# The first weight panel in two transfers, and the first product ahead of the second half of x

## The reference

```python
h = rmsnorm(x, norm_mix[0])
b_gate, c_gate, u = jnp.split(h @ w_in, 3, axis=-1)    # w_in: 1024 x 3072
v = c_gate * u
conv = causal convolution of v over 3 tokens
x = x + (b_gate * conv) @ w_out
```

## Time and profile before

| what | value |
|---|---|
| median of 3 runs | 1274.33 us (1272.78 to 1274.46) |
| profiled execution, its own time | 1270.87 us |
| its span in the trace | 1269.1 us |
| TensorE busy | 1236.7 us, 97% of the span |
| VectorE, ScalarE busy | 1001.9 us, 844.2 us |
| bytes moved | 325.22 MB, mean 256 GB/s |

### The profile page before, as it was taken

One profiled execution on the slowest core, in us unless ns is written; L12 is line 12 of the kernel. 1 busy time (PEld: TensorE's weight loads), 2 busy tenths in 40 slices (PEclk: granted clock), 3 DMA queues, 4 the chain that ended last, 5 costly groups with the idle time before them and its releaser, 6 DMA issues.

```text
span 1269.1 us, 18118 instructions
## 1 busy us (share of the span) xinstructions
PE 1236.7 (97%) x5924; PEld 1015.1 (80%) x5924; DVE 1001.9 (79%) x1397; ACT 844.2 (67%) x1218; POOL 39.0 (3%) x47
## 2 busy tenths in 40 slices
PE   7999999999998999999999999999997999999998
PEld 6878888888777787888788888888786877888887
DVE  6577555556977899999999999999999787766664
ACT  5656444446755788888888888888886587544442
POOL 0000000000100000000000000000100121000000
PEclk9999999999999999999999999999999999999999
DMA  9744555554233699999999999989998433455540
GB/s 357 276 162 170 195 187 181 194 198 166 68 133 133 257 369 378 363 361 370 362 376 372 357 376 374 375 344 370 375 422 301 166 140 115 165 182 196 175 156 34
DMA packets 48196, 325.22 MB, mean 256 GB/s; under 512 B 5416, under 2 KB 6704, under 8 KB 9872
## 3 DMA queue, kind: packets, MB, share of 16 engines
q1 hardware_dynamic: 44704, 316.40, 66.4%
q10 hardware_dynamic: 2752, 5.77, 1.2%
q0 software_dynamic: 688, 2.36, 0.5%
HBM read 318.74 MB, written 5.77 MB: 256 GB/s over the span
## 4 chain that ended last, share of the span: by engine, by line
PE 89%; DVE 5%; ACT 3%; issue 1%; POOL 0%; DMA 0%; SPq 0%; DVEq 0%; ACTq 0%
PE bank L431 25%; PE bank L433 25%; PE bank L432 25%; PE bank L1135 4%; PE bank L1136 2%; DVE wl L1812 2%; PE bank L495 2%; ACT wh L1193 1%; PE bank L842 1%; PE bank L467 1%; PE bank L697 1%; PE bank L1134 1%; PE bank L696 1%; DMA x<-x_dram 0%; DVE xt L1832 0%
## 5 line engine op out<-in xcount | busy, mean ns | idle before, releaser
L1812 DVE TENSOR_TENSOR wl<-raw,wh 128x1024 fp32r<-128x1024 f32 x598 | 714.5, 1219 | 180.3 <-ACT wh L1193 170.3
L1193 ACT ACTIVATE wh<-raw 128x1024 fp32r<-128x1024 f32 x598 | 630.5, 1058 | 278.2 <-PE bank L433 239.5
L431 PE MATMUL bank<-wh,xt 128*128 128x512 f32 (+2 forms) x1026 | 406.4, 396 | 6.6 <-DVE xt L1832 2.5
L433 PE MATMUL bank<-wh,xt 128*128 128x512 f32 (+2 forms) x1026 | 397.1, 387 | 0.0
L432 PE MATMUL bank<-wl,xt 128*128 128x512 f32 (+2 forms) x1026 | 396.5, 386 | 0.0
L431 PEld LDWEIGHTS bank<-wh,xt 128*128 128x128 f32 x1026 | 193.1, 188 | 45.5 <-DVE xt L1832 3.2
L433 PEld LDWEIGHTS bank<-wh,xt 128*128 128x128 f32 x1026 | 192.9, 188 | 40.3
L432 PEld LDWEIGHTS bank<-wl,xt 128*128 128x128 f32 x1026 | 193.4, 189 | 36.1
L431 PE MATMUL bank<-wh,hth 128*128 128x512 f32 x472 | 186.4, 395 | 1.0 <-DVE htl L1880 0.4
L433 PE MATMUL bank<-wh,htl 128*128 128x512 f32 x472 | 184.7, 391 | 0.0
L432 PE MATMUL bank<-wl,hth 128*128 128x512 f32 x472 | 184.3, 390 | 0.0
(11 more groups left out here) (304 smaller groups left out, 822.6 us busy)
## 6 DMA issues: line engine op xcount, KB each, us to landing
raw<-weights_dram SPq DMA_DIRECT2D x299, 1024.0 KB, 5.2
expert_results<-wide ACTq DMA_DIRECT2D x7, 512.0 KB
x<-x_dram SPq DMA_DIRECT2D x2, 512.0 KB, 7.3
wide<-bias_scratch ACTq DMA_DIRECT2D x8, 128.0 KB, 4.0
out_dram<-x SPq DMA_DIRECT2D x4, 256.0 KB, 2.0
fixed<-fixed_dram SPq DMA_DIRECT2D x1, 536.0 KB, 11.2
bias_scratch<-act ACTq DMA_DIRECT2D x2, 256.0 KB, 8.5
bias_scratch<-hbuf ACTq DMA_DIRECT2D x2, 256.0 KB, 14.9
```

Of the source, the lines that this page charges most:

```text
L431: mm(o, lh, wh[:, wi, sl], start=start, stop=False)
L433: return mm(o, ll, wh[:, wi, sl], start=False, stop=stop)
L1193: A(wh[:, c % SPLIT, 0:n], raw[:, (c // 2) % RAW, (c % 2) * UNIT:(c % 2) * UNIT + n], ACT.Copy).then_inc(hi_done, 1)
L1812: V.tensor_tensor(wl[:, c % SPLIT, 0:n], raw[:, (c // 2) % RAW, (c % 2) * UNIT:(c % 2) * UNIT + n], f32(wh[:, c % SPLIT, 0:n]), ALU.subtra ...
```

## The change

Panel 0 comes in two transfers of one unit each, unit 0 ahead of unit 1, both ahead of the second half of x. The first counts on the semaphore `stored`, which is otherwise used at the end alone, and whose last wait rises from 64 to 80. ACT makes hi(0) ahead of all pieces of x, and DVE lo(0) as well. TensorE makes product(0) between the rest of the bias and the transposes of the second half of x.

```diff
@@ sync
-            sp.dma_start(raw[:, 0, :], weights[0]).then_inc(raw_full[0], 16)
+            sp.dma_start(raw[:, 0, 0:UNIT], weights[0][:, 0:UNIT]).then_inc(sem("stored"), 16)
+            sp.dma_start(raw[:, 0, UNIT:2 * UNIT], weights[0][:, UNIT:2 * UNIT]).then_inc(raw_full[0], 16)
...
-            sp.wait_ge(sem("stored"), 64)
+            sp.wait_ge(sem("stored"), 80)
@@ tensor
-            turn_half("mix0", 1, 6)
...
-                chunk512(U_IN + 4 * j, 0, bank[2 * (j % 3):2 * (j % 3) + 2], normed("mix0") if j == 0 else None)
+                chunk512(U_IN + 4 * j, 0, bank[2 * (j % 3):2 * (j % 3) + 2], normed("mix0") if j == 0 else None,
+                         {0: lambda: turn_half("mix0", 1, 6)} if j == 0 else {})
@@ scalar
-                sc.wait_ge(raw_full[(c // 2) % RAW], 16 * (c // ROUND + 1) + 16 * i)
+                if c:
+                    sc.wait_ge(raw_full[(c // 2) % RAW], 16 * (c // ROUND + 1) + 16 * i)
...
             sc.wait_ge(sem("cols_in"), 32)
+            sc.wait_ge(sem("stored"), 16)
+            split_hi(0, 0)
             for c in range(4):
                 turned_hi_pair("mix0", 2 * c, 4 + c)
-                split_hi(c, 0)
+                if c > 0:
+                    split_hi(c, 0)
@@ vector
             dv.wait_ge(sem("cols_in"), 32)
+            split_lo(0, 0)
             for c in range(4):
...
-                split_lo(c, 0)
+                if c:
+                    split_lo(c, 0)
```

## The result

The changed kernel took 1275.83 us, median of 20 runs (1273.07 to 1381.28), the kernel before 1272.72 us, median of 20 (1271.12 to 1274.91). The ratio is 1.0024, 95% interval 1.0017 to 1.0031: 3.1 us slower. One of the 20 runs, the one of 1381.28 us with a granted clock of 0.849, is a slow run and is left out of the ratio. Two more sets of timed runs gave 1.0027 (1.0017 to 1.0038) and 1.0034 (1.0017 to 1.005).

What follows compares the result with a forecast made beforehand. TensorE, busy 1236.7 of 1269.1 us, bounds the kernel, with lo(6) only 0.91 us early at product(6). Delayed ACT and DVE work costs 1.80 us; 1274.33 + 1.80 = 1276.1 us, range 1273.1 to 1279.0.

Steps and rivals of the forecast that it cites:

- a new wait of TensorE for lo(6): At product(6), about 32 us: late ACT and DVE work leaves TensorE idle 1.5 us; loss 1.80 us.
- The level: Whole kernel: the 1.80 us loss added to a before-median of 1274.33 us gives 1276.1 us.
- Unit 0's landing: Start transfers: unit 0 alone lands at 9.7 us, 1.25 behind x's first half at 8.47.
- product(0): TensorE's first product starts at about 13.0 us, after a new wait of 0.45 behind the bias.
- The clock: TensorE during product(0): the clock rises at 16.15 us as before, so product(0) ends at 17.2.
- the late: Rival at product(0): clock stays low throughout it; +3.5 us, 1277.8 us; chance 0.20.
- the early rival: Rival at product(0): clock rises with its start, near 13.0; +0.3 us, 1274.6 us; chance 0.15.
- the distance of 0.43 going on past 16.2: Sign against the forecast: TensorE matmuls still 0.43 us apart, at half clock, after 16.2 us.
- The chain: ACT and DVE from the sixth transpose, 17.85 us, through hi(2), lo(2), angles and sine to lo(6)'s end, 33.42.
- The wait at product(2): TensorE, ready at 20.79 us, waits for lo(2) until 21.0: 0.25 us idle.
- the sum at product(6): TensorE ready at 31.92 us starts at 33.45: 1.5 us idle, 1.80 lost against 31.65 before.
- TensorE's own account: At the start, 0.45 us idle and slow matmuls offset 1.03 saved on transposes: worth nothing on TensorE alone.

Runs made afterwards that it cites:

- e1: The changed kernel run again with no edit, against the kernel before: ratio 1.0027 (1.0017 to 1.0038).
- e12: The changed kernel run a third time with no edit, against the kernel before: ratio 1.0034 (1.0017 to 1.005).
- e5: The kernel before run again with no edit, for a second trace: ratio 0.9995 (0.9986 to 1.0003).
- e2: The changed kernel with hi(6), hi(7), lo(6), lo(7) made ahead of squares, angles and sine: ratio 0.9999 to the kernel before.
- e7: The kernel before with three matmuls of zeros added on TensorE, two before the bias and one behind its first rows: ratio 0.9999.
- e8: e2 with the three added matmuls of zeros of e7: ratio 1.0002 (0.9994 to 1.0011) to the kernel before.
- e9: The kernel before with panel 0 in two transfers and nothing else changed: ratio 0.9998 (0.9988 to 1.0008).
- e10: The changed kernel with all transposes put back ahead of product(0), second run of that edit: ratio 0.9992 (0.9983 to 1.0001) to the kernel before.

## Why the prediction was right, point by point

The forecast was 1276.1 us in a range of 1273.1 to 1279.0; measured were 1275.8, 1276.0 and 1276.0. The mechanism, a new wait of TensorE for lo(6), forecast from 31.9 to 33.45 us and measured from 33.00 to 34.19 (32.12 to 33.29 in e1), was the one forecast. The size of the loss was not: 1.80 us forecast, 3.1 measured.

- *The level.* That the forecast lies within 0.3 us of the measured medians is luck. It stood on 1274.33, the median of three runs; twenty runs of the same kernel have 1272.72, 1.6 us less, and the loss on top came out 1.3 us more. The two errors cancel. From the better level the same sum gives 1274.5, which is in the range too.
- *Unit 0's landing.* Forecast 9.7, measured 3.07 + 6.34 = 9.41. What I had missed is that x's first half lands earlier too, 0.3 to 0.6 us; unit 0 came 1.28 us behind it (8.13 to 9.41), as the 1.25 of the sum. The rule of the Trainium skill, "DMA: Bandwidth & Descriptors", section on bandwidth, against transfers below 1 MiB is not borne out here: the second half of the panel landed at 3.58 + 7.1 = 10.7 us, the whole panel before at 10.97. The estimate by a straight line between that page's figures was also worked out wrong: it comes to 3.38 us for 512 KB and 0.6 more for two halves, not 3.3 and 0.4. Nothing in the forecast rests on it.
- *product(0).* Forecast 13.0 behind an idle 0.45; measured 12.78 behind 0.57. The bias had moved up with x, the operands had not moved as far.
- *The clock.* I took 16.15, as before; it was 17.5 in this trace, 15.6 and 17.8 in the next two. Neither the late nor the early rival came out, but something between them in each execution, and before varies in the same way. That a rise from one trace stands for the kernel was the weak point of the sum; it cancelled in the difference, since both kernels pay about the same for a late rise. One of my own signs of being wrong, the distance of 0.43 going on past 16.2, did come up in this trace and in e12. It was a bad sign: it takes one trace's rise for a property of the kernel, and in e5 the kernel before goes past 16.2 as well.
- *The chain.* From the sixth transpose to the end of lo(6) I had 15.57 us (0.09 + 1.80 + 0.03 + 5.32 + 8.33); measured 34.14 - 18.64 = 15.50. The wait at product(2) was forecast 0.25 and is 0.26. That these terms were read from rows of before, work by work, is why they held.
- *The step that was mis-sized* is the sum at product(6). I had 1.5 us of idle time and 1.80 of loss. Measured is 1.19 idle, and a restart: the first matmul behind it takes 0.50 instead of 0.23 until the next one, 0.27 more. The earlier trace rows have 0.23 there, since TensorE had not stopped. The idle time is shorter than forecast because TensorE came there later itself, 1.35 us behind instead of 0.27, by the late rise and by the restarts at product(0) and product(2). A loss of 2.0 to 2.2 us at equal rise of the clock is what the landmark shows, 0.2 to 0.4 above my 1.80. Nobody waits a second time, and the shift stays, as forecast: it is 2.81 us at the second matmul of product(6) (34.69 against 31.88) and 2.82 at the landmark.
- *The rest of the 3.1.* At the level of all runs about 1 us is left. The mean granted clock of each run, which counts the half-clock start as full and so speaks of later stretches, points to where: over 33 runs of the changed kernel it is 0.99636, over the 99 of before that have it on record 0.99707, 0.0007 less. A straight line through time against clock has a slope of about 850 us in both kernels, so this is some 0.6 us (an estimate), and at an equal clock the changed kernel is 2.6 us slower. That is the 2.2 of the landmark and 0.4, for which a rise that is later on average would do (17.5, 15.6 and 17.8 against 16.2 and 17.2), but three traces and two do not show that. The difference of the clocks is only about twice its own uncertainty, e12's trace shows no more slow stretches than the others, and no run isolates it. I leave open whether the change makes slow stretches after 360 us more frequent.
- *The chances.* I gave 0.28 to slower by over 0.2%; the ratio of 1.0024 lies there, with an interval that reaches below the bound. The likelier case, 0.68 for within 0.2%, did not come because of those 0.2 to 0.4 us, most of it restart, and the 1 us that stays open.
- *TensorE's own account* (nothing to be had by doing product(0) first) held to about half a microsecond: e2, with the wait for lo(6) gone, is at 0.9999, and its landmark 0.6 us behind. It still has the two early waits, 0.55 and 0.26 us, and a restart behind each; I had the waits at 0.45 and 0.25 and the restarts at nothing.

## What to carry to other kernels

An operation moved later on the busiest engine moves all that other engines do behind its result. Before moving it, follow that chain to the next place where the busy engine needs something from it, and compare its slack there (0.9 us here) with the delay; the engine's own sum, which came to zero, does not show it. If the move is wanted all the same, take long serial work that nobody needs soon out from in front of the operands: e2 did that with two loop bounds.

## What the runs showed of the hardware

- The clock rose from 1.2 to 2.4 GHz at 15.1 to 19.6 us, at different times in executions of the same kernel; in e7 TensorE was busy from 1.46 us on and the rise came at 16.7, in e8 the same first work had it at 4.7, and the clock was at half again from 11.5 to 18.3.
- Between 360 and 425 us, in work that no edit touches, there were two half-clock stretches in the first trace of the changed kernel, in e1 and in e5, none in before, e7, e9 and e10 and one in each of the others.
- The first 128x512 matmul behind a stop of 0.23 to 1.19 us took 0.47 to 0.50 us at full clock instead of 0.23.
- The added matmuls of zeros in e7 kept TensorE busy for 5.9 us (3.78 and 2.08) and moved the turning of x by 0.5 us, and the ratio is 0.9999 (0.9989 to 1.0010).
- A transfer landed earlier when the one behind it on the queue was cut in two: x's first half in 5.2 to 5.6 us instead of 5.8 to 5.9 (e7 and e8 left aside, 6.4 and 5.9). The issues behind it were also 0.5 us later; no run tells the two apart.
